# Delta-rule and attention decoder step: ones-matmuls on rounded pairs, q left unnormalised, mask inside the exponent, low products at the end of each weight chunk

## The reference, cut to what matters

```python
q = l2_normalize(q) * 128 ** -0.5        # q * rsqrt(sum(q*q) + EPS) / sqrt(128)
k = l2_normalize(k)
decay = where(incl, exp(where(incl, gc_i - gc_j, 0)), 0)   # incl: i >= j
a_mat = where(strict, (k*beta) @ k.T * decay, 0)
t_mat = inverse(a_mat + eye)
intra = q @ k.T * decay
# per chunk of 128 here: v_new = u - w @ S;  o = q_dec @ S + intra @ v_new
# S = S * exp(gl) + k_dec.T @ v_new
o = rms_norm(o, gnorm) * silu(z)         # o * rsqrt(mean(o*o) + EPS)
y = o @ w_out
```

## Time and profile before

| | before |
|---|---|
| median of 3 runs | 2893.99 us (2893.37 to 2894.33) |
| the profiled execution's own time | 2895.47 us |
| its span | 2893.6 us |
| TensorE busy | 2870.3 us, 99% of the span |
| VectorE busy | 1795.9 us, 62% |
| ScalarE busy | 1418.8 us, 49% |
| GpSimd busy | 193.8 us, 7% |
| granted TensorE clock, mean | 0.998 |
| one DeltaNet turn (step 1 to step 1) | 52.30 us |

### The profile page before, as it was taken

One profiled execution on the slowest core, in us unless ns is written; L12 is line 12 of the kernel. 1 busy time (PEld: TensorE's weight loads), 2 busy tenths in 40 slices (PEclk: granted clock), 3 DMA queues, 4 the chain that ended last, 5 costly groups with the idle time before them and its releaser, 6 DMA issues.

```text
span 2893.6 us, 68883 instructions
## 1 busy us (share of the span) xinstructions
PE 2870.3 (99%) x25543; PEld 2794.9 (97%) x25543; DVE 1795.9 (62%) x2868; ACT 1418.8 (49%) x2139; POOL 193.8 (7%) x301
## 2 busy tenths in 40 slices
PE   8999999999999999999999999999999999999999
PEld 7999999999999999999999999999999999999999
DVE  6778788788886455555555444577555555554444
ACT  6656566566564444444444344566444444444343
POOL 0212222122220000000000000000000000000000
PEclk9999999999999999999999999999999999999999
DMA  7666656656555556555555555744455555555554
GB/s 217 181 183 182 192 169 181 192 159 191 170 177 191 192 186 182 178 178 180 181 178 180 180 182 178 219 152 132 168 177 181 181 179 178 180 181 180 178 181 147
DMA packets 521090, 518.97 MB, mean 179 GB/s; under 512 B 32127, under 2 KB 444200, under 8 KB 520664
## 3 DMA queue, kind: packets, MB, share of 16 engines
q1 hardware_dynamic: 519150, 510.34, 56.9%
q0 software_dynamic: 1152, 5.58, 0.6%
q10 hardware_dynamic: 594, 0.25, 0.0%
HBM read 492.12 MB, written 32.82 MB: 181 GB/s over the span
## 4 chain that ended last, share of the span: by engine, by line
PE 67%; DVE 1%; ACT 1%; issue 0%; DMA 0%; DVEq 0%; ACTq 0%
PE bank L484 11%; PE bank L486 11%; PE bank L485 11%; PE upper L486 11%; PE upper L484 11%; PE upper L485 11%; PE upper L1013 0%; ACT w_hi L465 0%; PE upper L1037 0%; PE upper L1025 0%; DMA x_res<-x_spill 0%; DVE w_lo L472 0%; PE upper L1014 0%; PE upper L1150 0%; ACT scores L798 0%
## 5 line engine op out<-in xcount | busy, mean ns | idle before, releaser
L472 DVE TENSOR_TENSOR w_lo<-w_raw,w_hi 128x1024 fp32r<-128x1024 f32 x858 | 1049.7, 1223 | 933.5 <-ACT w_hi L465 929.0
L465 ACT ACTIVATE w_hi<-w_raw 128x1024 fp32r<-128x1024 f32 x858 | 908.8, 1059 | 1263.5 <-PE bank L486 736.0
L484 PE MATMUL bank<-h_hi,w_hi 128*128 128x264 f32 x3168 | 937.1, 296 | 3.4 <-DVE w_lo L472 3.4
L485 PE MATMUL bank<-h_lo,w_hi 128*128 128x264 f32 x3168 | 901.1, 284 | 0.0
L486 PE MATMUL bank<-h_hi,w_lo 128*128 128x264 f32 x3168 | 900.4, 284 | 0.0
L484 PEld LDWEIGHTS bank<-h_hi,w_hi 128*128 128x128 f32 x3168 | 598.0, 189 | 24.6 <-issue 12.1
L485 PEld LDWEIGHTS bank<-h_lo,w_hi 128*128 128x128 f32 x3168 | 598.8, 189 | 1.3
L486 PEld LDWEIGHTS bank<-h_hi,w_lo 128*128 128x128 f32 x3168 | 597.3, 189 | 0.0
L484 PE MATMUL upper<-h_hi,w_hi 128*128 128x264 f32 x1456 | 415.3, 285 | 0.0
L486 PE MATMUL upper<-h_hi,w_lo 128*128 128x264 f32 x1456 | 414.2, 284 | 0.0
L485 PE MATMUL upper<-h_lo,w_hi 128*128 128x264 f32 x1456 | 413.5, 284 | 0.0
(11 more groups left out here) (429 smaller groups left out, 4057.3 us busy)
## 6 DMA issues: line engine op xcount, KB each, us to landing
w_raw<-in_w_gate_up_dram SPq DMA_DIRECT2D x704, 256.0 KB, 2.9
w_raw<-in_w_in_a_dram SPq DMA_DIRECT2D x388, 256.0 KB, 3.2
w_raw<-in_w_down_dram SPq DMA_DIRECT2D x352, 256.0 KB, 2.9
w_raw<-in_w_out_a_dram SPq DMA_DIRECT2D x128, 256.0 KB, 3.1
s_dec<-in_state_delta_dram SPq DMA_DIRECT2D x32, 512.0 KB, 5.7
out_dram<-s_dec SPq DMA_DIRECT2D x32, 512.0 KB, 5.0
w_raw<-in_w_q_b_dram SPq DMA_DIRECT2D x64, 256.0 KB, 3.2
w_raw<-in_w_o_b_dram SPq DMA_DIRECT2D x64, 256.0 KB, 2.9
```

Of the source, the lines that this page charges most:

```text
L465: nc.scalar.activation(w_hi[:, s % SPL, :], w_raw[:, s, :], ACT.Copy).then_inc(hi_ready, 1)
L472: ops.tensor_tensor(w_lo[:, s % SPL, :], w_raw[:, s, :], w_hi[:, s % SPL, :].bitcast(F32), ALU.subtract).then_inc(lo_ready, 1)
L484: nc.tensor.matmul(bank[bk][:, 0:T], wh, xh, start=first, stop=False)
L485: nc.tensor.matmul(bank[bk][:, 0:T], wh, xl, start=False, stop=False)
```

## The change

1. **q is not normalised.** `qk_sq` [128, 2, 264] goes, and `k_sq` [128, 264] takes its place: only k is squared, summed, logged and exponentiated, and VectorE's multiplication (L2262) covers 264 columns in place of 528. To keep EPS right, the sum under the root of the outputs gets a term in q's squares: ScalarE squares q at step 13, scaled by P x EPS^0.5, VectorE adds it to the outputs' squares at n = 21, and the bias of the outputs' logarithm becomes EPS^2 x P.
2. **k's sum from two rounded parts.** ScalarE rounds k's squares (`k_hl[:, 0]`), VectorE subtracts to get the rest (`k_hl[:, 1]`, at n = 19), and TensorE sums both with a float32r matrix of ones: two float32r products in place of two float32 ones.
3. **The outputs' sums from rounded parts too.** After VectorE's addition of q's term, ScalarE rounds the sums (`sums_hi`, n = 21, before its two small operations), VectorE subtracts after its eight state updates (`sums_lo`, end of n = 21), and TensorE's step 23 has four float32r products in place of two float32 ones. It waits for `on_added`, that is for VectorE's subtraction.
4. **The mask in the exponent.** A tile `floor` holds 0 where incl is 1 and a very negative number elsewhere; VectorE's ET operation (L2258) takes the minimum with it rather than with 0, in another form of instruction (two tensor inputs and a scalar). The exponential is then 0 outside incl, and GpSimd's `masked_decay` goes; intraT is computed from ET.
5. **Low products last.** In `tiles`, the first half of a chunk has the 8 high products of its 4 tiles; the second half has the 8 of the other 4 tiles, and then all 8 low products. The wait for the low part moves behind the high products. A step in the middle of a chunk thus stands behind 8 products in place of 12, and before 16. Where `ends` is given the old order stays.

The core of the diff:

```diff
         def tiles(pe, c, tl, part=None, ends=None):
...
+            high = lambda t: w_hi[:, s % SPL, t * P:(t + 1) * P]
+            low = lambda t: w_lo[:, s % SPL, t * P:(t + 1) * P]
...
             if part in (None, 0):
+                pe.wait_ge(hi_ready, 4 * q + (s + 1))
+            for t, bk, xh, xl, first, last in tl if part is None else tl[4 * part:4 * part + 4]:
+                nc.tensor.matmul(bank[bk][:, 0:T], high(t), xh, start=first, stop=False)
+                nc.tensor.matmul(bank[bk][:, 0:T], high(t), xl, start=False, stop=False)
+            if part in (None, 1):
                 pe.wait_ge(lo_ready, 4 * q + (s + 1))
...
+                for t, bk, xh, xl, first, last in tl:
+                    m = nc.tensor.matmul(bank[bk][:, 0:T], low(t), xh, start=False, stop=last)
                 m.then_inc(w_used, 1)
```

```diff
-            def masked_decay(g):
-
-                pool.wait_ge(et_exp, 3 * g + 1)
-                after(pool, seq_pe, 7 * (g - 1) + 6)
-                pool.tensor_tensor(intraT[:, :, :], ET[:, :, :], bc(incl, 1, 4), ALU.mult).then_inc(incl_ready, 1)
```

ScalarE:

```diff
-                nc.scalar.activation(qk_sq[:, :, :], qk[:, :, :], ACT.Square).then_inc(sq_ready, 1)
+                nc.scalar.activation(k_sq[:, :], qk[:, 1, :], ACT.Square).then_inc(sq_ready, 1)
+                act.wait_ge(sq_ready, 3 * g + 1)
+                nc.scalar.activation(k_hl[:, 0, :], k_sq[:, :], ACT.Copy).then_inc(sq_ready, 1)
...
-                    for i in range(2):
-                        nc.scalar.activation(qk_sq[:, i, :], B[i][:, 0:T], ACT.Ln, bias=bias_c[:, 0:1]
-                                             ).then_inc(rn_ln, 1)
-                    act.wait_ge(rn_ln, 2 * g + 2)
-                    nc.scalar.activation(qk_sq[:, 0, :], qk_sq[:, 0, :], ACT.Exp, bias=bias_c[:, 1:2], scale=-0.5
-                                         ).then_inc(rn_ready, 1)
-                    nc.scalar.activation(qk_sq[:, 1, :], qk_sq[:, 1, :], ACT.Exp, scale=-0.5).then_inc(rn_ready, 1)
+                    nc.scalar.activation(k_sq[:, :], B[0][:, 0:T], ACT.Ln, bias=bias_c[:, 0:1]).then_inc(rn_ln, 1)
+                    act.wait_ge(rn_ln, g + 1)
+                    nc.scalar.activation(k_sq[:, :], k_sq[:, :], ACT.Exp, scale=-0.5).then_inc(rn_ready, 1)
...
+                elif n == 13:
+                    after(act, on_added, 2 * G)
+                    nc.scalar.activation(q_sq[:, :], qk[:, 0, :], ACT.Square, scale=float(P * EPS ** 0.5)).then_inc(q_sq_ready, 1)
...
+                elif n == 21:
+                    act.wait_ge(on_added, 2 * G + 1)
+                    nc.scalar.activation(sums_hi, sqn[:, :, :], ACT.Copy).then_inc(on_sq, 1)
```

TensorE:

```diff
-                    pe.wait_ge(on_sq, G + 1)
-                    pe.wait_ge(rn_ln, 2 * min(G + 1, GROUPS - 1) + 2)
+                    pe.wait_ge(rn_ln, min(G + 1, GROUPS - 1) + 1)
+                    pe.wait_ge(on_added, 2 * G + 2)
                     for i in range(2):
-                        m = nc.tensor.matmul(B[i][:, 0:T], ones, sqn[:, i, :], start=True, stop=True)
+                        nc.tensor.matmul(B[i][:, 0:T], ones_r[:, :], sums_hi[:, i, :], start=True, stop=False)
+                        m = nc.tensor.matmul(B[i][:, 0:T], ones_r[:, :], sums_lo[:, i, :], start=False, stop=True)
...
-                for i in range(2):
-                    m = nc.tensor.matmul(B[i][:, 0:T], ones, qk_sq[:, i, :], start=True, stop=True)
-                m.then_inc(ss_ready, 1)
+                nc.tensor.matmul(B[0][:, 0:T], ones_r[:, :], k_hl[:, 0, :], start=True, stop=False)
+                nc.tensor.matmul(B[0][:, 0:T], ones_r[:, :], k_hl[:, 1, :], start=False, stop=True
+                                 ).then_inc(ss_ready, 1)
```

VectorE:

```diff
-                    ts(ET[:, m_, :], gcb[:, h, c * P:(c + 1) * P], sc_g[:, m_:m_ + 1], 0.0, ALU.subtract,
-                       ALU.min).then_inc(et_pre, 1)
+                    stt(ET[:, m_, :], gcb[:, h, c * P:(c + 1) * P], sc_g[:, m_:m_ + 1], floor[:, :], ALU.subtract,
+                        ALU.min).then_inc(et_pre, 1)
+                elif n == 19:
+                    dve.wait_ge(sq_ready, 3 * g + 2)
+                    tt(k_hl[:, 1, :], k_sq[:, :], k_hl[:, 0, :].bitcast(F32), ALU.subtract).then_inc(sq_ready, 1)
...
-                    tt(qk[:, :, :], qk[:, :, :], qk_sq[:, :, :], ALU.mult).then_inc(qn_ready, 1)
+                    tt(qk[:, 1, :], qk[:, 1, :], k_sq[:, :], ALU.mult).then_inc(qn_ready, 1)
...
+                    if n == 21:
+                        dve.wait_ge(on_sq, 2 * G + 1)
+                        dve.wait_ge(q_sq_ready, G + 1)
+                        tt(sqn[:, :, :], sqn[:, :, :], bc(q_sq[:, :], 1, 2), ALU.add).then_inc(on_added, 1)
...
+                    if n == 21:
+                        dve.wait_ge(on_sq, 2 * G + 2)
+                        tt(sums_lo, sqn[:, :, :], sums_hi.bitcast(F32), ALU.subtract).then_inc(on_added, 1)
```

More of the change, by code:

```diff
@@ L226, in yoco_step @@
                 kq_rows = st_("kq_rows", [P, 2, P])
+                q_sq = st_("q_sq", [P, T])
+                ones_r = st_("ones_r", [P, P], F32R)
+                floor = st_("floor", [P, P])
+                k_hl = st_("k_hl", [P, 2, T], F32R)
                 kv_pad = st_("kv_pad", [P, 3, 96])
@@ L351, in yoco_step @@
         sq_ready = sem("sq_ready")
+        q_sq_ready = sem("q_sq_ready")
+        on_added = sem("on_added")
         ss_ready = sem("ss_ready")
@@ L1466, in first_turn @@
                 strict_beta(0)
-                masked_decay(0)
                 pool.dma_start(conv_s[0, :, 0:2, :], state_conv[0, :, 1:3, :]).then_inc(stored, 16)
@@ L1486, in turn @@
                             strict_beta(g)
-                        elif j == 11:
-                            masked_decay(g)
             first_turn()
@@ L1535, in _ @@
             split_hi(act, first_chunk(0))
+            act.wait_ge(masks_in_s, 16)
+            nc.scalar.activation(ones_r[:, :], ones, ACT.Copy).then_inc(aux_copied, 1)
+            nc.scalar.activation(floor[:, :], incl, ACT.Copy, bias=MASKED, scale=-MASKED).then_inc(aux_copied, 1)
             act.wait_ge(consts_set, 2)
@@ L2460, in first_turn @@
                     else:
-                        for n in (10, 11, 12, 13, 23):
+                        for n in (10, 11, 12, 13, 19, 23):
                             early(0, n)
```

58 lines of the change are left out of this document (30 added, 28 removed).

## The result

The changed kernel takes 2908.73 us (median of 5 runs, 2906.80 to 2910.77) against 2894.33 us of the kernel before (5 runs, 2893.37 to 2895.37). The ratio is 1.005, with a 95% interval of 1.0036 to 1.0063: slower by over 0.2%, as forecast, and within 4 us of the predicted 2905. The profiled execution took 2906.8 us, its span is 2905.0.

A forecast was written before the change was run, and what follows sets the result against it. TensorE's issue time bounds each turn, with side chains' slack deciding: turns +12.0 us, last turn +0.7, prologue -1.5, rest 0, in all +11.2 us, giving 2905 us against the 2894.0 median; range 2882 to 2917.

The forecast's parts named there:

- TensorE's saving of 1.1 us: Per turn: cheaper outputs' sums 0.41 us, q and k sums 0.65, a late start some 0.07; if all else stays covered.
- The outputs' sums at 804.0: TensorE's outputs' sums wait for k's logarithm until about 804.0, VectorE's subtraction just behind at 803.62; without waits, 802.85.
- Steps 15 and 19: Mid-chunk steps wanted 0.49 us sooner; waits for ScalarE's copy lose 0.2 us, for VectorE's dec_sel 0.26 us.
- Step 5: TensorE step waiting for VectorE's Xm, forecast to end at 815.81 for 815.46; start 815.87, before 815.73.
- The sum for a turn: Waits outweigh TensorE's 1.1 us saving: a turn takes 0.8 us longer; 15 such turns add 12.0 us.
- The prologue: Before the turns: waits for low parts vanish, taken as -2.3 us; first turn's k remainder costs 0.8; net -1.5 us.
- FFN: same products, 0: FFN stage: no mid-chunk step and same products, so no change; prices changing with product order were ruled out.
- w_o: no step in a chunk's middle: Output projection w_o: no mid-chunk steps and same products, so a change of 0.
- The mask: Without GpSimd's masked_decay, VectorE gets 1.03 us back before a turn's last split; only part is of use.
- The covers hold: Rival, 0.22 faster: outer products, sums and step 5 on time; turn -0.65 us, 2883, or 2876 if steps 15, 19 hold.
- The mask doesn't free VectorE: Rival: tap slow for another reason, split starts at 799.8, 0.7 us more a turn, 2916; within the 0.62 for slower.
- Half of it: Rival, 0.16 same: one chain holds for most of its length, waits and savings cancel; 2894 us, within 5.

The follow-up runs named there:

- two edits: Middle step after 12 products, q's term by TensorE: bank 1's sums first, 2890.89 us; changed kernel with qdec behind Xm, 2907.45 us; both edits on the former base, 2882.92 us.
- that kernel: The kernel before with only the new order of products (low products last), GpSimd's mask kept: 2923.42 us, ratio 1.0095, turns of 54.65 us.

## Why the prediction was right, and where it was off

**What bounds the kernel.** Right. A TensorE without waits had next to no room, and each chain's slack was what had to be read. The kernel with the mask's removal alone shows it from the other side: a microsecond less for VectorE, and nothing gained.

**TensorE's saving of 1.1 us.** Nearly right: 1.0. The price of 0.90 for the float32 sums, read from 908.46 to 909.48, has in it the slow start of the weight product behind them (0.32 us to the next one, for 0.12). At the outputs' sums that is right, and it shows as 24 products that take 2.91 us for 3.11. Behind the sum for q and k an outer product comes first, and 0.53 is saved, not 0.65.

**The outputs' sums at 804.0, held by k's logarithm.** Right: 803.96 with the logarithm's end 0.05 ahead. The outer product's wait was right too. Step 1 was given for 807.4 and came at 807.46.

**Steps 15 and 19.** Step 15: 0.2 predicted, 0.19 measured. Step 19: 0.26 predicted, 0.37 measured. The wait itself fits, as the product starts at 795.35 in the time of before (given: 795.37). The rest is a slower restart: from this product to the next weight product TensorE takes 0.47 us, not 0.36.

**Step 17** isn't in the prediction. It loses 0.10 us. The prediction looked for steps with less than 0.49 us of room, and this one escaped it.

**Step 5.** From step 1 (0.20 ahead) to step 5 (0.14 behind) the prediction had a growth of 0.34 us, and it was 0.47. Xm ends at 815.97 instead of 815.81.

**The sum for a turn**, 0.8 us, is thus the term that was mis-sized: it measured 1.12. Of the missing 0.3 us, 0.1 is each of step 17, the restart at step 19, and step 5. All are restarts and small waits, for which the bounds had room (1.6 to 1.9 us a turn at the far end). Over 15 turns it is 4.8 us: up to the first product of w_out the profiled executions differ by 15.8 us, where the sum had 10.5 (12.0 less 1.5).

**The prologue.** The first turn is ahead by 1.2 us at step 1, for 1.5 predicted.

**The rest of the program** was put at 0, and there two steps of the prediction fail. I laid the two kernels on each other chunk by chunk, by the starts of ScalarE's rounding where it waits for TensorE. The changed one is 16.3 us late at the end of w_out, 13.8 at the start of w_o, 14.7 behind its first eight chunks, and 12.8 near the end of the second FFN.

"FFN: same products, 0" is wrong, and with it the sentence that rules out a price by the order of products. A chunk of gate and up takes 2.919 us for 2.924, one of the first down projection 2.918 for 2.932, with no wait in either: about 4 us less over both FFNs. Stretches of equal length in the first FFN, gate and up and then down, hold more products now (length, busy PE and its products, and so on). Before:

```profile
1200.00:1550.00 350.00, 350.00 (x2878) 350.00 (x2877) 187.38 (x210) 142.66 (x150) 0.00 (x0) 1.00 0.58 180
1600.00:1800.00 200.00, 200.00 (x1640) 200.00 (x1639) 96.44 (x101) 80.22 (x84) 0.00 (x0) 1.00 0.53 181
```

And now:

```profile
1200.00:1550.00 350.00, 350.00 (x2882) 350.00 (x2882) 187.41 (x211) 143.24 (x150) 0.00 (x0) 1.00 0.59 180
1600.00:1800.00 200.00, 200.00 (x1647) 200.00 (x1646) 97.29 (x102) 81.41 (x85) 0.00 (x0) 1.00 0.53 181
```

All eleven kernels with the low products last have 1646 to 1648 products in the second stretch and the three in the old order 1639 or 1640, at a granted clock of 1.00 in each. The kernel before with the new order alone has it too, so it is the order's.

"w_o: no step in a chunk's middle" is wrong as well. The program has `attention(8 + j // 4, 2 * (j % 4) + 1)` between the halves of w_o's first eight chunks. Two waits of TensorE came there that the kernel before doesn't have at this length, and 1.0 us is lost:

```profile
PE upper L1051 <- ACT f_sq L823: 0.5, 1, 0.5
PE upper L1088 <- ACT pdT L843: 0.4, 1, 0.4
```

**Luck.** The sum had +11.2 us, and the profiled executions differ by 11.3 (2906.8 less 2895.47). That is closer than the terms deserve. The turns are 5 us worse and w_o 1 us; the FFNs give 4 back. The last 1.7 come from the end of the program: behind the start of the last chunk's rounding the profiled execution takes 15.3 us before and 13.6 now, with a granted clock of 0.78 (so for a part of it at the lower of its two levels) and of 1.00 in the second half of that. The kernel with the mask's removal alone takes 16.9 there, so this belongs to the execution and not to the change. The medians differ by 14.4.

**The mask.** The prediction gave its removal 1.03 us of VectorE's time, part of it of use. The tap did become 0.48. But its true worth in the changed kernel, 1.09 us a turn, lies elsewhere: without the removal `dec_sel` would have collided, and that I hadn't seen. I had priced the mask by where it stands in the trace of before, after an order change that moves what releases it. The prediction came out right because both parts were in the change. Of the order alone I would have said 2899 to 2904, and it is 2923.

**The rivals.** *The covers hold* needed both chains 1.1 us shorter. They were not, not even in the old order. *The mask doesn't free VectorE* is refuted by the tap's 0.48. *Half of it*, no change, is what the old order shows (2898.26, waits and savings cancel), but not the changed kernel: its interval of 1.0036 to 1.0063 excludes it. The range of 2882 to 2917 held these outcomes and no change at all, so that the time lies in it says little; the direction, and the turns of 53.42 for 53.1, are what bear the forecast out.

**What stays open.** The growth of step 17 was read from positions and not tried by itself. Why a chunk of 24 products takes 5 to 14 ns less with its low products last, without a wait in either order, no run here tells.

## What to carry to other kernels

Before you save work on an engine that never waits, find the operation at the end of each chain that runs beside it. If its slack (the time by which it is done before it is needed) is a few tenths of a microsecond, a cheaper product only waits there, and the operations that make it cheap (a rounding, a subtraction) lengthen the very chain. A reordering within a chunk is not free even with the same products: it moves each step that stands in the middle of it, so keep the step at its place and move only the products (that alone turned 14 us lost into 3 to 4 won). When you list those steps, search the program for them in every stage: w_o was put at 0 here as it "had none", and it had them in eight chunks. Where a move gives nothing, look for the second wait behind it: two edits that each give 0 to 0.2 us gave 0.46 together.

## What the runs showed of the hardware

- VectorE's `dec_sel`, two operations of 128x8, takes 0.61 us alone and 1.70 when GpSimd's operation with two SBUF inputs starts together with the second of them. It ends 0.02 us after GpSimd does. The Trainium skill (SBUF — State Buffer, "SBUF: two separate sides") calls the shared ports "an exclusive lock, not a bandwidth split". Here the trace agrees, and even an operation of 128x8 is stopped.
- The same GpSimd operation on 128x512 took 1.27 us in that kernel, with VectorE stopped for it, and 2.14 in the kernel before. There it started 0.23 us after a split of VectorE, which took its usual 1.21 us:

```profile
795.24 1.21 DVE L472 TENSOR_TENSOR w_lo<-w_raw,w_hi 128x1024 fp32r<-128x1024 f32 x1
```

  So there GpSimd's operation, which came second, got longer first, and then the tap behind the split did. In the collision with `dec_sel` the two started within 0.02 us of each other, and VectorE was the one that waited.
- The products behind float32 sums start more slowly than those behind float32r sums: 24 weight products took 3.11 us and 2.91. In the kernel before, 0.20 of that lies in the first of them. What in the engine makes it so no run here tells.
- A chunk of 24 float32r products takes 2.924 us (gate and up) or 2.932 (down) with high, high, low for each weight tile, and 2.919 or 2.918 with the 8 low products last, at a granted clock of 1.00 and without waits.
- TensorE restarts more slowly after a short wait: from the four products of `dec_sel` to the next weight product it is 0.36 us where they came without one, and 0.47 where they waited.
